# The last block's attention scores as four fp32r matmuls: query parts stacked, keys in a high and a low part

## The reference

```python
HEAD_DIM = 64
NSA_KV_HEADS = 2
q = rms_norm(q, q_gain)          # 8 heads, 4 for each key head
k_s, k_w = rms_norm(k_s, k_gain), rms_norm(k_w, k_gain)
scores = q @ k.T * HEAD_DIM ** -0.5 + bias    # then a masked softmax
```

## Time and profile before

| | |
|---|---|
| median of 3 runs | 1943.89 us (1943.64 to 1944.12) |
| profiled execution, its own time | 1943.84 us |
| its span, first to last instruction | 1942.4 us |
| PE busy | 1936.6 us, 100% of the span |
| PE weight loads | 1649.1 us, 85% |
| DVE busy | 1336.7 us, 69% |
| ACT busy | 1000.7 us, 52% |
| granted TensorE clock | 1.00 in every stretch |

### The profile page before, as it was taken

One profiled execution on the slowest core, in us unless ns is written; L12 is line 12 of the kernel. 1 busy time (PEld: TensorE's weight loads), 2 busy tenths in 40 slices (PEclk: granted clock), 3 DMA queues, 4 the chain that ended last, 5 costly groups with the idle time before them and its releaser, 6 DMA issues.

```text
span 1942.4 us, 25506 instructions
## 1 busy us (share of the span) xinstructions
PE 1936.6 (100%) x10030; PEld 1649.1 (85%) x10030; DVE 1336.7 (69%) x1963; ACT 1000.7 (52%) x1433; POOL 0.2 (0%) x4
## 2 busy tenths in 40 slices
PE   9999999999999999999999999999999999999999
PEld 7889988988888888898888888888888888888887
DVE  6756778887545557898688877589666444666654
ACT  5645555675556544575565655444444334444442
POOL 0000000000000000000000000000000000000000
PEclk9999999999999999999999999999999999999999
DMA  8555325455553455545534345555555555555562
GB/s 328 176 193 174 131 90 192 174 199 187 191 189 133 174 192 195 182 177 207 211 116 149 128 152 195 196 194 177 191 195 200 197 201 192 190 189 194 185 228 109
DMA packets 51707, 353.23 MB, mean 182 GB/s; under 512 B 5652, under 2 KB 7196, under 8 KB 9860
## 3 DMA queue, kind: packets, MB, share of 16 engines
q1 hardware_dynamic: 50016, 348.84, 50.2%
q10 hardware_dynamic: 1572, 2.75, 0.4%
HBM read 349.47 MB, written 2.11 MB: 181 GB/s over the span
## 4 chain that ended last, share of the span: by engine, by line
PE 93%; DVE 5%; ACT 1%; issue 1%; DMA 0%; ACTq 0%; DVEq 0%
PE bank L1197 92%; DVE WL L2121 2%; DVE AR L2298 0%; ACT WH L1624 0%; DVE ft L2882 0%; DVE AR L2411 0%; DVE XP L2294 0%; DVE AR L2408 0%; DVE XP L2396 0%; PE bank L1342 0%; DMA X<-in_x 0%; DVE AR L2287 0%; PE bank L1427 0%; DVE AR L2322 0%; DVE AR L2321 0%
## 5 line engine op out<-in xcount | busy, mean ns | idle before, releaser
L1624 ACT ACTIVATE WH<-raw 128x1024 fp32r<-128x1024 f32 x649 | 683.4, 1057 | 645.1 <-PE bank L1197 639.0
L2121 DVE TENSOR_TENSOR WL<-raw,WH 128x1024 fp32r<-128x1024 f32 x649 | 784.0, 1221 | 316.4 <-ACT WH L1624 313.1
L1197 PE MATMUL bank<-XP,WH 128*128 128x512 f32 (+2 forms) x1584 | 498.6, 389 | 0.6 <-DVE WL L2117 0.3
L1197 PE MATMUL bank<-WH,FP 128*128 128x512 f32 x1408 | 434.7, 389 | 0.1
L1197 PEld LDWEIGHTS bank<-XP,WL 128*128 128x128 f32 x1504 | 281.8, 187 | 59.4 <-issue 0.7
L1197 PEld LDWEIGHTS bank<-WH,FP 128*128 128x128 f32 x1408 | 264.3, 188 | 56.1 <-DVE WL L2121 1.0
L1197 PE MATMUL bank<-XP,WL 128*128 128x256 f32 (+1 forms) x1504 | 308.5, 279 | 0.1
L1197 PE MATMUL bank<-WH,XP 128*128 128x512 f32 (+1 forms) x960 | 301.2, 389 | 0.3 <-DVE WL L2121 0.3
L1197 PE MATMUL bank<-WL,FP 128*128 128x512 f32 x704 | 273.9, 389 | 0.0
L1197 PEld LDWEIGHTS bank<-XP,WH 128*128 128x128 f32 (+1 forms) x1584 | 248.1, 187 | 7.5 <-issue 1.4
L1197 PE MATMUL bank<-WH,AP 128*128 128x512 f32 x704 | 217.2, 389 | 0.0
(11 more groups left out here) (336 smaller groups left out, 1616.9 us busy)
## 6 DMA issues: line engine op xcount, KB each, us to landing
raw<-in_W SPq DMA_DIRECT2D x326, 1024.0 KB, 4.8
out<-XT ACTq DMA_DIRECT2D x8, 256.0 KB, 2.0
raw<-in_W SPq DMA_DIRECT2D x3, 512.0 KB, 6.7
X<-in_x SPq DMA_DIRECT2D x3, 512.0 KB, 12.6
AR<-rv SPq DMA_DIRECT2D x1, 1024.0 KB, 5.9
cst<-in_cst SPq DMA_DIRECT2D x1, 899.5 KB, 11.7
raw<-in_W SPq DMA_DIRECT2D x2, 256.0 KB, 4.3
AR<-in_sgu SPq DMA_DIRECT2D x1, 512.0 KB, 5.7
```

The costliest lines, as they stand in the source:

```text
L1197: return pe.matmul(o, lhsT, rhs, start=start, stop=stop)
L1624: ac.activation(w_slot(WH, s), raw_half(hf), ACT.Copy).then_inc(s_hi, 1)
L2121: tt(w_slot(WL, s), raw_half(pl.half_of[s]), w_slot(WH, s).bitcast(F32), ALU.subtract).then_inc(s_lo, 1)
```

## The change

The query of each head is split: its high part (fp32r copy by ACT, "q high") goes to the 64 rows in which the head lies, its low part (DVE: query less high part, "q low") to the other 64 rows of a 128x256 array QS, of which there are two in turn. The keys are made once: KN is the normalised key array of both heads (now written by full 128-row instructions), KH0 and KH1 hold the high part of one key head twice, in both halves of rows ("k high", four ACT copies of 64x512), KL holds the low parts, 64 rows for each key head ("k low", two DVE subtractions). a0 is four fp32r matmuls: the stacked query by KH (both parts of the query times the high key, 128 rows) and the high query by KL (64 rows), for each of the two banks. The clearing of the unused key rows falls away; only the 32 columns of kcz are still cleared.

In the list of steps, "k high" stands at the end of section d behind "hi 310", "k low" ahead of "cmp gelu"; q high and q low of head 0 stand behind d5 of heads 6 and 7 of "stick"; those of head h+1 directly behind a0 of head h, for h = 0 to 6. q high of head h waits for a0 of head h-2, which read the same QS; q low waits for q high; a0 waits for q low.

```diff
@@ -655,7 +655,7 @@
              23: [("qk rstd", 1)], 25: [("qk scaled", 1), ("qk squares", 2)], 27: [("zeros", 2), ("qk rstd", 2)],
-             29: [("qk scaled", 2)]}
+             29: [("qk scaled", 2)], 30: ["k high"]}
     for at in range(31):
@@ -669,6 +669,8 @@
     for step in (("nsa gates", 0), ("cmp gelu", 0), ("zeros", 3), ("zeros", 0)):
+        if step[0] == "cmp gelu":
+            say("k low")
         say(*step)
@@ -700,8 +702,11 @@
         say("d5", h)
+        if h == 6:
+            say("q high", 0)
         if h == 7:
             say("sg gelu", 0)
+            say("q low", 0)
@@ -751,6 +756,9 @@
         say("a0", h)
+        if h < 7:
+            say("q high", h + 1)
+            say("q low", h + 1)
@@ -763,7 +771,7 @@
     wos = fill()
-    p.pipe(8, ["a0", a1, "a2", "a3", "a4", "a5", "a6", a7], wos, 46, (6, 1, 4, 0), (7, 6, 5, 1, 4, 3, 2, 0),
+    p.pipe(8, [a0, a1, "a2", "a3", "a4", "a5", "a6", a7], wos, 46, (6, 1, 4, 0), (7, 6, 5, 1, 4, 3, 2, 0),
            [4] * 6 + [3] * 2 + [5] * 4 + [6] * 3)
@@ -1013,8 +1021,10 @@
-        KZ = ar(5120, 544)
-        kswn, kcz = [ar(5120, 512), blk(RAW, 6, 2)], ar(5632, 32)
+        kcz = ar(WK + 5976, 32)
+        KN, KL = blk(RAW, 6, 2), ar_r("KL", 7680, 512)
+        KH = [ar_r(f"KH{g}", 5120 + 512 * g, 512) for g in range(2)]
+        QS = [ar_r(f"QS{i}", 13824 + 256 * i, 256) for i in range(2)]
         kcn_, sqk_ = kcn[:, 0:15], sqk[:, 0:15]
@@ -1111,6 +1121,8 @@
         s_cz = sem("s_cz")
+        s_kh, s_kl, s_qh, s_ql = (sem("s_" + n) for n in ("kh", "kl", "qh", "ql"))
@@ -1559,12 +1571,16 @@
                     if h == 0:
-                        pe.wait_ge(s_qsc, 4)
-                    q = blk(QZ, h % 4)
-                    k = kswn[h // 4]
-                    mm(X1[:, 0:512], q[:, 128:256], k, True, True)
-                    mm(Y1[:, 0:256].rearrange("p (s k) -> p s k", s=2), q[:, 0:128],
-                       k.rearrange("p (s k) -> p s k", s=2)[:, :, 0:128], True, True).then_inc(s_n1, 1)
+                        pe.wait_ge(s_kl, 2)
+                    pe.wait_ge(s_ql, h + 1)
+                    g = h // 4
+                    q, rows = QS[h % 2], slice(64 * g, 64 * g + 64)
+                    k, kl = KH[g], KL[rows, :]
+                    two = lambda ap: ap.rearrange("p (s k) -> p s k", s=2)
+                    mm(X1[:, 0:512], q[:, 128:256], k[:, :], True, False)
+                    mm(X1[:, 0:512], q[rows, 128:256], kl, False, True)
+                    mm(two(Y1[:, 0:256]), q[:, 0:128], two(k[:, :])[:, :, 0:128], True, False)
+                    mm(two(Y1[:, 0:256]), q[rows, 0:128], two(kl)[:, :, 0:128], False, True).then_inc(s_n1, 1)
                     free[3] = free[4] = s_n2s, h + 1
@@ -1947,6 +1963,12 @@
                     rstd(rs6, bank[7][:, :], 64, 0).then_inc(s_qrs, 1)
+                elif what == "k high":
+                    ac.wait_ge(s_qsc, 3)
+                    for g in range(2):
+                        for half in range(2):
+                            ac.activation(KH[g][64 * half:64 * half + 64, :], KN[64 * g:64 * g + 64, :],
+                                          ACT.Copy).then_inc(s_kh, 1)
                 elif what == "cmp gelu":
@@ -1963,6 +1985,13 @@
                     rstd(sqk_, bank[3][:, 256:271], 64, 0).then_inc(s_qrs, 1)
+            def q_high(h):
+                sl = slice(64 * (h // 4), 64 * (h // 4) + 64)
+                if h >= 2:
+                    ac.wait_ge(s_n1, h - 1)
+                ac.activation(QS[h % 2][sl, :], blk(QZ, h % 4)[sl, :], ACT.Copy).then_inc(s_qh, 1)
@@ -2004,6 +2033,8 @@
                     ac.activation(lA[h % 4], zA[h % 4], ACT.Exp).then_inc(s_g5e, 1)
+                elif what == "q high":
+                    q_high(n)
                 elif what == "sg gelu":
@@ -2629,7 +2662,7 @@
                     elif n == 2:
-                        dv.memset(KZ, 0.0)
+                        dv.memset(kcz, 0.0)
                         dv.memset(CZ, NEG)
@@ -2650,17 +2683,14 @@
                         src = blk(RAW, m)
-                        if m < 4:
-                            ins = stt(blk(QZ, m), src, pcol("q_gain", 0), rs6[:, j * T:(j + 1) * T], ALU.mult, ALU.mult)
-                        else:
-                            for half in range(2):
-                                sl = slice(64 * half, 64 * half + 64)
-                                ins = stt(blk(kswn[half], j)[sl, :], src[sl, :], pcol("k_gain", 0, sl),
-                                          rs6[sl, j * T:(j + 1) * T], ALU.mult, ALU.mult)
-                    if n == 2:
-                        chain(ins)
-                        ins = dv.memset(RAW[0:64, 6 * T:8 * T], 0.0)
+                        to, gain = (blk(QZ, m), "q_gain") if m < 4 else (blk(KN, j), "k_gain")
+                        ins = stt(to, src, pcol(gain, 0), rs6[:, j * T:(j + 1) * T], ALU.mult, ALU.mult)
                     ins.then_inc(s_qsc, 1)
+                elif what == "k low":
+                    dv.wait_ge(s_kh, 4)
+                    for g in range(2):
+                        sl = slice(64 * g, 64 * g + 64)
+                        tt(KL[sl, :], KN[sl, :], KH[g][sl, :].bitcast(F32), ALU.subtract).then_inc(s_kl, 1)
                 elif what == "cmp out":
@@ -2677,6 +2707,12 @@
+            def q_low(h):
+                sl, to = slice(64 * (h // 4), 64 * (h // 4) + 64), slice(64 - 64 * (h // 4), 128 - 64 * (h // 4))
+                dv.wait_ge(s_qh, h + 1)
+                tt(QS[h % 2][to, :], blk(QZ, h % 4)[sl, :], QS[h % 2][sl, :].bitcast(F32), ALU.subtract).then_inc(s_ql, 1)
             def b_out(n):
@@ -2728,6 +2764,8 @@
                        czs.rearrange("p (s n) -> p s n", n=1).broadcast_to([128, 16, 15]), ALU.mult).then_inc(s_cz, 1)
+                elif what == "q low":
+                    q_low(n)
                 elif what == "d2":
```

## The result

The kernel after took 1948.13 us (median of 13 runs, 1947.86 to 1948.80); the kernel before, measured beside it, 1943.88 us (13 runs, 1943.55 to 1944.20). The ratio is 1.0022 with an interval of 1.0015 to 1.0029: 4.25 us slower. No run of one kernel reaches those of the other and the interval leaves out 1, so the slowdown is real, but at 0.22% it is about the 0.2% that the prediction takes as its limit for a difference that counts. The forecast was 1946.8 us, which is 2.9 us slower; the range reached to 1948.4, so the time lies inside it by 0.3 us.

The account below looks back on a forecast made before the run. DVE's full row, coupled with full PE, was taken to bound the attention stage: DVE's lateness of 4.61 us less 0.49 slack less 2 x 0.59 gives 2.94, so 1943.84 + 2.94 = 1946.8 us; range 1944.2 to 1948.4.

Parts of the forecast that it names:

- What bounds the stage: Attention stage, 1045 to 1075 us: PE and DVE both full and coupled twice per head, PE 0.1 to 0.7 us behind.
- The work ahead of the stage costs nothing: Key splits and head 0's query split, before the attention stage: costed at nothing; without cover up to 2.4 us.
- q low of head 1: On DVE ahead of sg norm, waiting for ACT's q high: sg norm starts 2.14 us late.
- The further q lows: On DVE's full row, heads 2 to 6: 0.45 us each, 0.56 behind the four products (heads 4, 6).
- a0(6): Score matmuls of head 6 on PE: start at 1079.33 against 1075.21, 4.12 us late.
- The price of a0: Four fp32r matmuls per head on PE: 0.70 us instead of 1.29, saving 0.59 per head.
- The third rival: Each a0 on PE: row changes or weight loads not hidden, up to 0.76 us per head, 1948.3 us; 12%.
- PE's idle time: Before most a0 and before sg: PE's total idle time rises from 5.8 us to some 13.
- The change doesn't do what it says: a0's matmuls not at the fp32r rate: four records of over 0.4 us spacing; 2%.
- The gain goes through: DVE takes the extra work without pushing a0, so all 4.7 us are saved: 1939.1 us; 8%.

Follow-up runs that it names:

- early: The changed kernel with q high and q low of head 1 moved to the stage before, beside those of head 0; 1946.68 us.
- pool: The changed kernel with 128-row low-key matmuls, head 1's split moved to the stage before, and every q low on GpSimd instead of DVE; 1942.92 us.
- rows128: The changed kernel with its low-key matmuls contracting all 128 rows instead of the head's 64; 1946.75 us.
- grouped: The changed kernel with a0's matmuls reordered, both 128-row ones first, then both 64-row ones; 1947.40 us.
- before64: The kernel before with its two fp32 matmuls of a0 contracting only the head's own 64 rows; 1946.69 us.
- pool3: As pool, with the four products per head behind the softmax moved from DVE to GpSimd too; 1946.03 us (1944.39 to 1948.04).
- both: The changed kernel with 128-row low-key matmuls and head 1's split moved to the stage before; 1945.12 us.

## Why the prediction was right, and where it was not

In short: the direction, the engine that decides and the added work's price were right, the price of the new matmuls was not. The forecast of 2.9 us slower missed the measured 4.25, which lies outside the forecast's own bounds; it is inside the range only because a rival with 12% had widened that.

**What bounds the stage: right.** PE is full on the page and still not what sets the time up to head 6. In four kernels whose a0 costs 0.69, 1.09, 1.29 and 1.49 us, a0(6) is late by 3.75, 3.76, 3.76 and 3.77. So the row of DVE decides there.

**The work ahead of the stage costs nothing: right.** From 935 to 955 us ACT is busy for 13.24 us now, 2.44 more than in the earlier trace rows (2.4 forecast), DVE for 14.28, about as before, and a0(0) starts no later (1037.68, before 1037.82).

**q low of head 1: right, a little too large.** Forecast 2.14, measured 1.87. The wait, the q high (0.40) and the semaphore (0.04) came as worked out; ACT took up WH<-raw 0.11 us after the start of the root in front of it, where the earlier trace rows show 0.34, so q high was ready earlier. That is 0.23 of the 0.27. The prediction says that DVE waits only once, at 1081.05; it read over the 0.86 us for in_sgu in the earlier trace rows. This did the sum no harm, since q low of head 1 holds sg norm back beyond that landing, but it made early and pool come out worse than expected.

**The further q lows: right.** From sg norm to the end of the bias of head 5 (4.22 late, 4.36 after the shift of 0.14), 4.36 - 1.87 = 2.49 us were added; 3 x 0.45 + 2 x 0.56 = 2.47 were forecast. What follows a q low starts 0.45 or 0.46 us after it (1075.07 to 1075.52), and behind the four products it ends their overlap: from 1074.03 to 1075.52 it is 1.49 instead of the 0.93 of the earlier trace rows, so 0.56.

**a0(6): 3.77 late instead of 4.12,** which follows from the 0.27 above and from 0.1 us more slack.

**The price of a0: wrong, and this is the step that failed.** "Two of the four have only 64 contraction rows; no fp32r row of that kind exists, and I take them at the same price." They cost 1.49 us per head with their neighbours, not 0.70. Instead of giving back 2 x 0.59 at heads 6 and 7, a0 takes 2 x 0.20 more. The account is then: 4.12 - 1.18 = 2.94 forecast; 3.77 + 0.40 = 4.17 by the measured terms, a0(7)'s own slack left aside; 4.25 measured. The third rival named this mechanism with its place, the two heads that decide and 0.76 us per head if it is fully exposed; measured are 0.79. It got 12%, for the reason that "all loads of its tiles hide behind matmuls". They do, and those tiles never change the row count, so they were no evidence on it. The nearest rows were of another kind, and the bounds of the sum should have reached up to the 0.189 us of a load, for one matmul out of two at least. The forecast's own bounds, 1945.8 to 1947.3, covered DVE's uncertainty and left this one out; the range held the time only because the rival had widened it.

**PE's idle time: wrong for the same reason.** The forecast wanted 13 us of it; span less busy time gives 7.5. PE had nothing saved to wait with. Of the 4.1 us that the span grew, eight a0 dearer by 0.20 make 1.6; the 2.5 that are left must be waits. The starts show these better than the brackets do: the matmul in front of a0(6) starts at 1077.93, its successor would follow 0.23 later, and a0(6) starts at 1078.84, a stall of 0.68 where the bracket says 0.52; and a matmul that has waited is itself 0.07 longer.

**"The change doesn't do what it says": excluded,** by rows128, where the four matmuls run at the fp32r rate. **"The gain goes through": excluded for this order of work,** by pool: even with all added work gone from DVE it is 1.0 us, not 4.7.

## What to carry to other kernels

When two engines are both full in a stage and hand banks to each other, a cheaper instruction on one is worth only the slack, plus what comes after the last handover; work added to the other is paid in full beyond that slack. Before an instruction is called free to start sooner, look at what it waited for: behind the engine that is taken away may stand a transfer. Price a matmul with its neighbours: a shape that the stream doesn't hold otherwise, such as 64 rows among 128, costs at the change in and out, and rows that are all of one shape say nothing on it. Where a forecast assumes such a price, its range should run from the nearest row to that row plus a weight load.

## What the runs showed of the hardware

- One stretch of 64-row matmuls among 128-row ones costs 0.40 us more than the same at 128 rows, in fp32r (0.69, 1.09, 1.49 us for none, one and two stretches: rows128, grouped, after) and in fp32 (1.29 to 1.69 us: before, before64). The last 0.10 of each lies in the matmul behind it, whose record is 0.50 instead of 0.40 us long.
- Four fp32r matmuls with 128 rows, two over 512 and two over 256 columns, take 0.69 us; the two fp32 ones that they replace, over 512 and 256 columns, take 1.29.
- A weight load of 64 rows behind a matmul of 128 starts with its own matmul (1038.00 and 1038.01 in after); the same load with 128 rows starts one matmul ahead (1037.72 and 1037.95 in rows128).
- A subtraction of 64x256 that starts on other partitions than its neighbours takes 0.45 us of DVE's row (after, 1075.07 to 1075.52). GpSimd takes 0.72 to 1.89 us for the same, in pool and pool3.
- A product with a column of scalars is recorded on GpSimd (pool3) for 1.31 us over 256 columns and 0.89 over 128, on average; on DVE (before) for 0.35 and 0.28.
- Two elementwise products of 128x256 on DVE took 0.52 and 0.60 us beside a running GpSimd instruction (pool), 0.42 without one (both).
